# Another order of decoding items, and the output product in pieces among head pairs, in a hybrid attention step

## The reference

```
P = x @ w_in                       # latent query, latent kv, rope key, NSA query, three kv pairs, gates, two SiLU gates
o_lat = softmax(q_lat . latent rows + q_rope . rope keys) @ latent rows          # MLA, 8 heads
o_cmp = softmax(q . compressed keys) @ compressed values                         # NSA branch 1, also ranks the blocks
o_sel = softmax(q_rot . keys of the chosen blocks) @ their values                # NSA branch 2
o_win = softmax(q_rot . keys of the last 512) @ their values                     # NSA branch 3
mixed = concat(o_lat @ w_uv * silu(z_mla), (g0*o_cmp + g1*o_sel + g2*o_win) * silu(z_nsa))
y = layer_norm(ALPHA * x + mixed @ w_o)                                          # for 4 prompt tiles and the 32 new tokens
```

## Time and profile before

| what | before |
|---|---|
| median of 3 runs | 552.86 us (552.48 to 553.14) |
| the profiled execution's own time | 552.96 us |
| its span, first to last instruction | 550.9 us |
| TensorE busy | 478.3 us |
| VectorE, ScalarE, GpSimd busy | 211.8, 150.4, 124.2 us |
| mean granted TensorE clock | 0.943 |

### The profile page before, as it was taken

One profiled execution on the slowest core, in us unless ns is written; L12 is line 12 of the kernel. 1 busy time (PEld: TensorE's weight loads), 2 busy tenths in 40 slices (PEclk: granted clock), 3 DMA queues, 4 the chain that ended last, 5 costly groups with the idle time before them and its releaser, 6 DMA issues. The chain is left out here.

```text
span 550.9 us, 8511 instructions
## 1 busy us (share of the span) xinstructions
PE 478.3 (87%) x2940; PEld 277.0 (50%) x2940; DVE 211.8 (38%) x656; ACT 150.4 (27%) x415; POOL 124.2 (23%) x212
## 2 busy tenths in 40 slices
PE   6969899999999999899888796938899999595994
PEld 3434466637875545445535463424566665352441
DVE  0035402010123135634554665633356674434115
ACT  0061002011122014333334333233544462412000
POOL 0033454244444001111210110011444341110000
PEclk9988999999998999999799897888999999898798
DMA  8985507162549254000501648253180010010101
GB/s 282 321 253 170 152 1 211 32 170 76 175 122 375 79 190 189 2 1 1 154 1 52 256 140 251 70 168 104 65 334 20 2 49 1 27 50 0 76 1 76
DMA packets 49156, 64.69 MB, mean 117 GB/s; under 512 B 10362, under 2 KB 39546, under 8 KB 49018
## 3 DMA queue, kind: packets, MB, share of 16 engines
q1 hardware_dynamic: 48218, 63.10, 35.3%
q0 software_dynamic: 512, 1.05, 0.7%
q10 hardware_dynamic: 384, 0.01, 0.0%
HBM read 59.89 MB, written 8.41 MB: 124 GB/s over the span
## 5 line engine op out<-in xcount | busy, mean ns | idle before, releaser
L902 PE MATMUL psum<-wring,bufA 128*128 128x512 f32 (+1 forms) x192 | 73.5, 537 | 0.0
L1423 ACT ACTIVATE wring<-wring,small 128x128 f32<-128x128 f32 (+3 forms) x96 | 53.2, 555 | 70.2 <-DVE small L1622 70.0
L1969 POOL TENSOR_SCALAR wring<-wring,small,gate 128x128 f32<-128x128 f32 (+3 forms) x32 | 25.2, 787 | 186.4 <-DVE small L1740 186.3
L884 PE MATMUL psum<-bufA,wring 128*128 128x512 f32 x128 | 60.8, 626 | 0.8 <-DVE comp L1574 0.8
L1328 PE MATMUL psum<-ring,zsil 128*128 128x512 f32 x128 | 60.5, 630 | 0.0
L902 PEld LDWEIGHTS psum<-wring,bufA 128*128 128x128 f32 x192 | 36.7, 194 | 31.3 <-issue 28.3
L1622 DVE CUSTOM_DVE_ANT_0 wring<-psum,const 128x128 f32<-128x128 f32 (+3 forms) x96 | 43.8, 486 | 17.5 <-PE psum L1111 15.7
L1431 ACT COPY mid<-psum 128x512 f32<-128x512 f32 (+1 forms) x38 | 20.4, 538 | 78.8 <-PE psum L857 78.5
L1328 PEld LDWEIGHTS psum<-ring,zsil 128*128 128x128 f32 x128 | 25.4, 203 | 31.4 <-issue 31.4
L857 PE MATMUL psum<-const,wring 128*128 128x128 f32 x248 | 39.3, 288 | 2.1 <-DVE w1h L1675 1.4
L884 PEld LDWEIGHTS psum<-bufA,wring 128*128 128x128 f32 x128 | 24.7, 200 | 29.4 <-issue 29.3
(11 more groups left out here) (224 smaller groups left out, 655.4 us busy)
## 6 DMA issues: line engine op xcount, KB each, us to landing
ring<-in_cmp_pages SPq DMA_DIRECT2D x64, 128.0 KB, 2.3
wring<-in_w_in SPq DMA_DIRECT2D x3, 2048.0 KB, 9.0
ring<-in_mla_pages SPq DMA_DIRECT2D x40, 128.0 KB, 2.8
ring<-in_sel_pages SPq DMA_DIRECT2D x40, 128.0 KB, 2.4
ring<-in_win_pages SPq DMA_DIRECT2D x8, 512.0 KB, 7.6
ring<-in_w_om SPq DMA_DIRECT2D x1, 4096.0 KB, 13.5
out_s_win<-in_state_win_kv SPq DMA_DIRECT2D x1, 4064.0 KB
bufA<-in_x_t SPq DMA_DIRECT2D x8, 272.0 KB, 5.5
```

The costliest lines, as they stand in the source:

```text
L884: ins = pe.matmul(bank, wr[:, b % 2, k, c * P:(c + 1) * P], xT[:, k, 0:SEQ], start=(k == 0), stop=(k == KC - 1))
L902: ins = pe.matmul(bank[:, 0:w], xT[:, c, t * P:(t + 1) * P], wr[:, b % 2, c, 0:w], start=(c == 0), stop=(c == KC - 1))
L1423: ins = act.activation(p, p, ACT.Exp, bias=nmp[:, n % 4, g:g + 1], scale=-1.0, accum_out=lp[:, n % 4, g:g + 1])
L1969: ins = pool.tensor_scalar(p, p, c, gate3[:, i, at:at + 1], ALU.mult, ALU.mult)
```

## The change

The decoding items come in another order. The steps of the two compressed chains are spread over the bodies of `("win", 0)`, `("win", 1)` and `("mla", 1)`; before, each chain stood in one body. The step `omla` (before in the body of `("win", 0)`) and the four `vup` steps, the products L1282 (before in that of `("win", 1)`), now end the body of `("sel", 1)`. The first eight slot loads now bring the first MLA item and both window items; later slots are reloaded when an item's `pv` is done, four at a time for the MLA and the last selected item. Value products come four slots after the scores instead of three; posts of block 0 five products later, other posts two. The product of the output is cut into four parts for each half (two chunks of the contraction each), two parts after each MLA slot from the eighth on; it accumulates in the bank `O` (one bank), which is also that of `pv`. The last tile's second half is cut into two pieces of 256 columns. Roots come one slot, norms two and three slots after the statistics, the norm in two halves. The call that loads the square root's table is gone. MLA value products of all tiles use bank `V`. The pieces of x are issued by ACT's queue.

The diff, cut (the address and size of small buffers and some of SP's waits are left out):

```diff
-T_LAG, V_LAG = 3, 3
+T_LAG, V_LAG = 3, 4
...
-ITEMS = [("mla", 0), ("mla", 1), ("win", 0), ("win", 1), ("sel", 1), ("sel", 0)]
+ITEMS = [("mla", 0), ("win", 0), ("win", 1), ("mla", 1), ("sel", 1), ("sel", 0)]
...
-OUT_AT = {("mix", 0): 1, ("out", 0, 0): 4, ("out", 0, 1): 5, ("root", 0): 5, ("norm_y", 0): 6,
-          ("out", 1, 0): 8, ("out", 1, 1): 10, ("root", 1): 11, ("norm_y", 1): 11,
-          ("out", 2, 0): 12, ("out", 2, 1): 14, ("root", 2): 15, ("norm_y", 2): 15,
-          ("out", 3, 0): 16, ("out", 3, 1): 18}
+LAST = NT - 1
+
+
+def spans(n):
+
+    if n == 0:
+        return [(0, 256)]
+    return [(0, 512), (512, 1024)] if n < LAST else [(0, 512), (512, 768), (768, 1024)]
+
+
+def out_steps(n):
+
+    return [("out", n, k, part) for k in range(len(spans(n))) for part in range(4)]
+
+
+def out_after(at):
+
+    steps = [("mix", 0)] if at == 1 else []
+    if 2 <= at < 6:
+        steps.append(out_steps(0)[at - 2])
+    n, k = at // 4 - 1, at % 4
+    for done, last in ((0, 5), (1, 11), (2, 15)):
+        if at == last + 1:
+            steps.append(("root", done))
+        if at in (last + 2, last + 3):
+            steps.append(("norm_y", done, at - last - 2))
+    if 1 <= n < LAST:
+        steps += out_steps(n)[2 * k:2 * k + 2]
+    return steps
...
-        for lag in (2, 1):
-
-            if n >= lag and seq[n - lag][0] in posts and lag == 1 + (seq[n - lag][0] == B_MLA):
+        for lag in (NT, 2):
+
+            if n >= lag and seq[n - lag][0] in posts and lag == (NT if seq[n - lag][0] == B_MLA else 2):
                 now.append(("post", *seq[n - lag]))
...
-        g = {("mla", 1): 0, ("win", 1): 1}.get(x)
-        if g is not None:
-            drop = compressed(g)
-            body = body[:4] + drop[:2] + body[4:5] + drop[2:4] + body[5:6] + drop[4:]
+        c0, c1 = compressed(0), compressed(1)
         if x == ("win", 0):
+            body = (body[:1] + c0[:1] + body[1:2] + c0[1:2] + body[2:4] + c0[2:3] + body[5:] + c0[3:4] + body[4:5])
+        if x == ("win", 1):
+            body = (body[:2] + c0[4:5] + body[2:4] + c1[:1] + c0[5:6] + body[4:] + c1[1:2] + c0[6:])
+        if x == ("mla", 1):
+            body = (body[:1] + c1[2:4] + body[1:3] + c1[4:5] + body[3:] + c1[5:])
+        if x == ("sel", 1):
             body.append(([("omla",)], 1))
-        if x == ("win", 1):
             body += [([("vup", t)], .9) for t in range(PT)]
...
-        steps += [step for step, at in OUT_AT.items() if at == m - N_NSA]
-
-    steps += [("root", PT - 1), ("out", PT, 0), ("norm_y", PT - 1), ("out", PT, 1), ("root", PT), ("norm_y", PT)]
+        steps += out_after(m - N_NSA)
+
+    last = out_steps(LAST)
+    steps += [("root", LAST - 1)] + last[:4] + [("norm_y", LAST - 1, 0)] + last[4:8] + [("norm_y", LAST - 1, 1)]
+    steps += last[8:] + [("root", LAST), ("norm_y", LAST, 0), ("norm_y", LAST, 1)]
...
     if kind == "score":
         return BANKS_OF[a[0]]
-    if kind == "out":
...
 def o_uses(kind, *a):
-    if kind == "pvalue":
-        i, unit, x = UNITS[a[0]]
-        return int(spare_bank(i, unit) and x == 0)
+    if kind == "out":
+        return int(a[2] == 0)
...
     LOADS = [(("mla", 0, 0), 4, None), (("mla", 0, 1), 2, ("hid", 3)), (("mla", 0, 2), 3, ("hid", 3)),
-             (("mla", 0, 3), 0, ("chunks", PT)), (("mla", 1, 0), 1, ("chunks", PT)), (("mla", 1, 1), 7, ("hid", PT)),
-             (("mla", 1, 2), 5, ("proj", B_ZMLA)), (("mla", 1, 3), 6, ("proj", B_ZMLA)),
-             (("win", 0, 0), 2, ("mla", 0)), (("win", 0, 1), 3, ("mla", 0)), (("win", 1, 0), 0, ("mla", 0)),
-             (("win", 1, 1), 4, ("mla", 0)), (("sel", 1, 0), 5, ("mla", 1)), (("sel", 1, 1), 6, ("mla", 1)),
-             (("sel", 1, 2), 1, ("mla", 1)), (("sel", 1, 3), 7, ("mla", 1)), (("sel", 0, 0), 2, ("win", 0)),
-             (("sel", 0, 1), 3, ("win", 0)), (("sel", 0, 2), 0, ("win", 1)), (("sel", 0, 3), 4, ("win", 1))]
+             (("mla", 0, 3), 0, ("chunks", PT)), (("win", 0, 0), 1, ("chunks", PT)), (("win", 0, 1), 7, ("hid", PT)),
+             (("win", 1, 0), 5, ("proj", B_ZMLA)), (("win", 1, 1), 6, ("proj", B_ZMLA)),
+             (("mla", 1, 0), 4, ("mla", 0)), (("mla", 1, 1), 2, ("mla", 0)), (("mla", 1, 2), 3, ("mla", 0)),
+             (("mla", 1, 3), 0, ("mla", 0)), (("sel", 1, 0), 1, ("win", 0)), (("sel", 1, 1), 7, ("win", 0)),
+             (("sel", 1, 2), 5, ("win", 1)), (("sel", 1, 3), 6, ("win", 1)), (("sel", 0, 0), 4, ("mla", 1)),
+             (("sel", 0, 1), 2, ("mla", 1)), (("sel", 0, 2), 3, ("mla", 1)), (("sel", 0, 3), 0, ("mla", 1))]
...
-                sp.dma_start(xT[:, c, :], io["x_t"][:, c, :]).then_inc(x_in[c], 16)
...
-            held = [numbers(GB + b) for b in range(GB)]
             for x in LOADS[4:6]:
-                load_slot(*x, held)
+                load_slot(*x)
 
             sp.wait_ge(gate_done, NT)
...
             for x in LOADS[6:8]:
+                load_slot(*x)
+            held = [numbers(GB + b) for b in range(GB)]
+            for x in LOADS[8:16]:
                 load_slot(*x, held)
-
-            for x in LOADS[8:12]:
-                load_slot(*x)
-            early = [numbers(b) for b in range(GB // 2)]
-            for x in LOADS[12:16]:
+            held = [numbers(b) for b in range(GB)]
+            for x in LOADS[16:]:
                 load_slot(*x, held)
-            for x in LOADS[16:18]:
-                load_slot(*x, early)
-            late = [None] * (GB // 2) + [numbers(b) for b in range(GB // 2, GB)]
-            for x in LOADS[18:]:
-                load_slot(*x, late)
...
+                if n < LAST:
+                    sp.wait_ge(y_done, 2 * n + 2)
...
-                    n, half = a
-                    if step == ("out", 0, 0):
+                    n, k, part = a
+                    if step == ("out", 0, 0, 0):
                         pe.wait_ge(wo_in, 16)
                         for j in range(2):
                             wait_copied(pe, T, T.at("mix", n, j=j))
-                    elif n == 0:
-                        continue
-                    elif half == 0:
-                        for k in ("psel", "pmla"):
-                            wait_copied(pe, *value_bank(ORDER[n], k))
-                    u = A.at(*step)
-                    bank = claim(A, u)
-                    for c in range(KC):
+                    elif k == 0 and part == 0:
+                        for unit in ("psel", "pmla"):
+                            wait_copied(pe, *value_bank(ORDER[n], unit))
+                    u = O.at("out", n, k, 0)
+                    bank = claim(O, u) if part == 0 else bank_of(O, u)
+                    c0, c1 = spans(n)[k]
+                    for c in (2 * part, 2 * part + 1):
                         if n:
-                            ins = pe.matmul(bank, zT[:, c, ORDER[n] * P:(ORDER[n] + 1) * P],
-                                            wo[:, c, half * 512:(half + 1) * 512], start=(c == 0), stop=(c == KC - 1))
+                            ins = pe.matmul(bank[:, 0:c1 - c0], zT[:, c, ORDER[n] * P:(ORDER[n] + 1) * P],
+                                            wo[:, c, c0:c1], start=(c == 0), stop=(c == KC - 1))
                             continue
 
                         w = D_MODEL // 4
                         for j in range(4):
                             ins = pe.matmul(bank[j * NS_TOK:(j + 1) * NS_TOK, 0:w], mixT[:, c, :],
                                             wo[:, c, j * w:(j + 1) * w], start=(c == 0), stop=(c == KC - 1))
-                    ins.then_inc(A.full[u % A.n], 1)
+                    if part == 3:
+                        ins.then_inc(O.full[u % O.n], 1)
...
+            for c in range(KC):
+                act.dma_start(xT[:, c, :], io["x_t"][:, c, :]).then_inc(x_in[c], 16)
...
-                    ok(act.activation(warm[0:r], C("eps")[0:r, 1:2], ACT.Sqrt))
...
-                    n, half = a
+                    n, k, part = a
+                    if part < 3:
+                        continue
...
-                        bank = arrive(A, u)
+                    u = O.at("out", n, k, 0)
+                    bank = arrive(O, u)
...
+                        c0, c1 = 0, D_MODEL
+                    else:
+                        c0, c1 = spans(n)[k]
+                        ins = dve.scalar_tensor_tensor(out=y[:, c0:c1], in0=y[:, c0:c1], scalar=ALPHA,
+                                                       in1=bank[:, 0:c1 - c0], op0=ALU.mult, op1=ALU.add)
+                    ins.then_inc(O.free[u % O.n], 1)
+                    wait_copied(dve, O, u)
+
+                    w = 256 if n == LAST else 512
+                    for c in range(c0, c1, w):
+                        ok(dve.bn_stats(bnst[0:r, c // w, :], y[:, c:c + w]))
+                    if c1 == D_MODEL:
+                        dve.bn_aggr(bnag[0:r, n % 2, :], bnst[0:r, 0:D_MODEL // w]).then_inc(y_var, 1)
                 elif kind == "norm_y":
-                    n, r = a[0], rows(ORDER[a[0]])
```

(59 more changed lines are left out.)

11 lines of the change are left out of this document (2 added, 9 removed).

## The result

The changed kernel takes 543.71 us (median of 4 runs, 542.93 to 546.22); the kernel before, on the same chip, 552.67 (552.16 to 553.14). The ratio is 0.9846, 95% interval 0.9812 to 0.9879: 9 us faster, a little less than half of the forecast, at a time inside its range. The profiled execution has a span of 541.1 us, 9.8 less than before.

A forecast was written before the change was run, and what follows sets the result against it. TensorE, busy 87% of the span, was taken to bound the kernel, with its idle time and low clock. Terms from input to tail summed to -18.95 us: 552.96 to 534.0, 533.9 against the median; forecast 529 to 540, range 523 to 545.

The forecast's parts named there:

- Page waits: Decoding: waits of 3.1, 8.9 and 7.8 us for mla 1, sel 1 and sel 0, together 19.8 for 8.15: +11.6 us.
- three tail gaps: Last out product: pieces share one bank, so PE waits 0.95 us for each of out 4's three pieces, +2.85 us.
- Values and end together: Value products a slot later -7.5 us, output pieces and later roots and norms at the end -20.0, tail +2.1.
- The compressed chain: Decoding: chain cut into steps with other products between; waits 7.0 less 3.5, so -3.5 us, and low clock -2.2.
- The clock of the page stops: Decoding: two long page stops and a short one instead of one bring more low clock, +2.0 us.
- The order as a whole: Decoding: chain waits -3.5 and clock -2.2, page waits +11.6 and clock +2.0 us.
- The posts: Latent posts of block 0 behind the query block's products: removed 8.7 us, put back about 7.7, so -1.0.
- Input on two queues: Start: x pieces on ACT's queue let the first weight piece be issued one issue earlier, -0.45 us.
- rival 2: End keeps half its waits: VectorE late once per tile, one stop stays with its clock; +9, 543 us; chance 0.13.
- (1): Rival: pages come faster than one per half microsecond, 13.2 us less waiting, 521 us; chance 0.10.
- (3): Rival: posts come free, bias sums run before evict 4, no new stop; -6 for -1, 529 us; chance 0.11.
- (4): Rival: single out bank makes six pieces inside slots wait for VectorE; slower, 558 us at 4 us each; chance 0.06.

The follow-up runs named there:

- e6: Kernel before plus value products four slots after the scores and the whole output part (pieces, own bank, later roots and norms): 526.00 us, ratio 0.9530.
- e5: Kernel before with one change, value products four slots after the scores instead of three: 524.85 us, ratio 0.9511.
- e2: Changed kernel with the output product, roots and norms as before: 543.73 us, ratio 0.9837 to the kernel before.
- e3: Changed kernel with value products three slots after the scores, as before: 558.67 us, ratio 1.0110 to the kernel before.
- e13: Changed kernel, new order of items and loads kept, but each compressed chain in one body again: 544.98 us, ratio 0.9880 to the kernel before.
- e4: Changed kernel with the posts of the projections as early as before: 539.98 us, ratio 0.9785 to the kernel before.
- e9: Changed kernel plus products nobody reads (3, 8, 8 and 2) ahead of four waits, which stay: 533.56 us, ratio 0.9706 to the kernel before.
- e10: Changed kernel without the slot loads of the second MLA item and both selected items: 512.73 us, ratio 0.9306 to the kernel before.
- e14: Kernel before with value products a slot later, plus products nobody reads ahead of four waits, which stay: 519.54 us, ratio 0.9413.
- e1: Changed kernel with the decoding order, slot loads and places of the compressed chains as before: 527.32 us, ratio 0.9546 to the kernel before.
- e11: Kernel before plus value products a slot later and the later posts, nothing else: 527.93 us, ratio 0.9585.
- e7: Changed kernel, each page of the last selected item loaded in two transfers of 64 rows: 566.23 us, ratio 1.0266 to the kernel before.
- e12: Kernel before with value products a slot later, last selected item's last slot (8 pages) issued by ScalarE's queue: 529.56 us, ratio 0.9598.

## Where the prediction held and where it failed

- **Where the waits would be: right.** Page waits 3.5 + 8.0 + 7.9 = 19.5 us against 19.8; the post copies 6.0 against 5.6; three tail gaps of 0.87, 0.85 and 0.51 against 0.95 each; no idle time of L1177 in the end stretch.
- **Values and end together: right in sum, wrong in cause.** Forecast -7.5 - 20.0 + 2.1 = -25.4; e6 has -26.3. But the -20.0 was put down to the output pieces, and e5 and e2 show that the lag alone does it: with the lag the pieces are worth nothing, without it they remove the two long stops but leave 11.2 us of small waits (e3). The argument that a slot is longer than the copies was used for decoding and not for the end, where the same group of products waited.
- **The compressed chain: the step that failed.** Forecast -3.5 of waits and -2.2 of clock. The waits fell from 7.0 to 4.2, but the low clock did not fall with them: the stretches at 286.4 and 330.8 us hold 9.54 + 6.80 us of busy time, the three before (310.5, 334.4 and 341.3, of which the forecast left out the second) 3.50 + 3.40 + 5.25, so 8.2 us were lost instead of 6.1. Together -0.7 instead of -5.7, and e13, which prices the spreading itself, gives -1.9 with an interval of about 3 either way: the forecast lies outside it. Half of the low clock was taken to go because half of the waits went. The runs show that the slow work behind a stop is no fixed share of it: behind the same three waits at 282 us (1.36, 0.47 and 1.62 us) it is 9.54 us here, 5.2 in e4 and 3.2 in e9 and e10, and behind the chain's 2.78 us 6.80 here and none in e10. What sets it is open.
- **The clock of the page stops: mis-sized.** Forecast +2.0; behind the three stops 3.50 + 5.04 + 2.83 us of busy time ran at half the clock, 5.7 us lost against 1.5, so +4.2. e9 and e14 show that the stops bring it: with the stops filled it is gone, and the pages are loaded as before. The order as a whole was forecast at -5.7 + 13.6 = +7.9; the rows give 11.3 + 4.2 - 0.7 = +14.8, e1 measures 16.4.
- **The posts: wrong sign.** Forecast -1.0; +3.7 in e4, whose interval just misses the changed kernel's, and about +4 in e11, whose interval overlaps e5's a little. The stop was placed rightly and its clock too low (6.00 us of busy time at the low clock, 3.0 lost against the 2 taken), which makes +1.0; the rest is open.
- **Input on two queues: nothing that shows.** Forecast -0.45. The first weight piece was issued 0.45 us earlier (0.73 instead of 1.18 us), but PE's first product began at 4.80 us instead of 4.70. No run changes this part alone.
- **A reading.** Of the stretches in the earlier trace rows the first has a granted clock of 0.74, not 0.50 as the prediction says of all; only its idle time went into the sum.
- **The rivals.** The time is that of rival 2, by another way: the end kept no stop. The pages did not come faster (1), the posts were not free (3), and the single bank held PE up inside the slots only twice, by about 0.3 us each (4).

The parts measured alone make -26.3 + 16.4 + 3.7 = -6.2; the whole is -9.0. Each of these differences carries an interval of some 2 us, and parts that share a stop don't add up (e13).

## What to carry to other kernels

Ahead of any rebuilding, try one more stage of lag between the steps of a software pipeline whose buffers allow it: when an in-order engine waits for a copy, the cause of the lateness need not be removed if other work can stand in between. Price a stop by its length and by the slow work behind it, and don't scale the second with the first. A new order that takes away cover from transfers pays twice, and a wait removed ahead of a transfer's end is only handed on to it.

## What was not expected of the hardware

Products that nobody reads make the kernel faster: 19 us of them in waits that stay took 5.5 to 7.7 us off (e9), 11.3 us of them 5.4 us (e14). The slow work behind one and the same stop differs from run to run (3.2 to 9.5 us of busy time behind the waits at 282 us). Each half of a transfer cut in two by rows takes longer to issue than the whole (0.67 us against 0.55 for the page, e7), and two queues that each issue a page in half a microsecond landed 16 pages hardly sooner than one (9.6 us against 10.4 from the first issue to the score, e12 and e5).
